# A two-layer hybrid decoder trunk: the attention layer's loop over heads cut at another place, and the delta-rule layer without its products with the zero state

## The chip, the core and the metric

The kernel runs on one core of one Trainium2 chip. The metric is the device time of one execution in microseconds; the median of three runs is compared. One further execution was profiled, and all rows shown come from it.

## The reference

The input is 1024 tokens of width 1024, all float32. Two layers are computed, each of the form x = x + mixer(rms_norm(x)). Layer 0 is a gated delta rule with 8 heads (key width 128, value width 256): per head a state S of 128 x 256 runs over the sequence, and the first chunk starts from a state of zeros.

```python
def step(state, inp):
    q_c, k_c, u_c, w_c, g_c, qk_c = inp
    v_new = u_c - jnp.einsum("bhck,bhkv->bhcv", w_c, state)
    o = (jnp.einsum("bhck,bhkv->bhcv", q_c * jnp.exp(g_c)[..., None], state)
         + jnp.einsum("bhij,bhjv->bhiv", qk_c, v_new))
    state = (state * jnp.exp(g_last)[..., None]
             + jnp.einsum("bhck,bhcv->bhkv", k_c * ..., v_new))
    return state, o
state0 = jnp.zeros((Bn, H, DK, DV), f32)
```

Layer 1 is attention with 8 heads in three groups each (dilations 1, 4, 16; a window of 128 earlier keys in the dilated stream). Queries and keys are normalised and rotated, and the three groups of a position are merged by their softmax denominators, multiplied by silu(z), and projected out.

## The kernel before

The program runs in stages, one after the other: constants; the norm of layer 0; `delta_heads`; `out_projection` (p0); the norm of layer 1; `attention_heads`; `out_projection` (p1). Names in the trace carry the stage's letter: a_ for the delta-rule heads, b_ for the attention heads, p_ for the output projections. Float32 products of the projections are made of three products of rounded halves (`three_passes`, L336): high weight by high and by low activation, low weight by high activation.

In both head stages each engine has its own instruction list, written by a function `body(m, n)` that is called once for every head: in one body the projections of head n are made, and beside them the mixing of head m = n - 1, whose projections the body before made. The body is cut into slots (`for s in range(...)`). A slot holds a third of a half: 8 of the 24 matmuls that project 512 tokens for one unit of 128 columns. What else an engine does in a slot is fixed by tests on s. The first body has no head m, the last has no head n; those between are a hardware loop.

**Delta-rule heads.** A head has 8 tiles of 128 tokens, T = 8. Tile t takes slots 7 + 3t to 9 + 3t (`CHAIN0` = 7). In the first slot TensorE makes two products with the state (L754, into `step`), VectorE makes the residual `r` (L920) and ScalarE keeps the product with the query (`o1`, L622). In the second TensorE makes `new` (L763), and ScalarE makes `vn` (L627). In the third TensorE makes the state's update (L767, `kd` by `vn`) and the output within the tile (L768), and VectorE makes the next state (L929) and the output (L934). After the last tile VectorE clears the state (L927). Between them stand the steps of a block inverse (`first`, L850; `lev`, L857), for which GpSimd makes `um` (L537).

**Attention heads.** A head has 10 units (B_UNITS): a query and a key unit for each of three groups (units 0 to 5, 12 halves), three value units (6 to 8) and the gate z (unit 9). A body has 60 slots of projection. A query/key half q is projected in slots 3q to 3q + 2 and then goes through ScalarE and VectorE: ScalarE copies and squares it (L1483, L1485, L1488) in slot 3q + 3, VectorE splits the squares (`sq_lo`, L1706) and rotates in slot 3q + 4, TensorE sums the squares (L1609) at the end of slot 3q + 5, ScalarE makes the root in slot 3q + 6, and VectorE scales the half (`qk`, L1742) in slot 3q + 7. TensorE's list waits in its place: its sum of half q waits for `sq_lo` of that half.

For head m the same body has:

- slots 0 to 11: 12 pairs of score tiles on TensorE (L1568, into three buffers `ring`), and on VectorE for each tile the mask and the row maximum (L1659);
- slot 12: SyncE sends the maxima of two groups through device memory (`maxima`, L1388 to L1394) to bring them into token order; slot 17: VectorE joins them (L1665), SyncE sends them back (L1398 to L1402);
- slots 22 to 33: 24 exponentials on ScalarE (L1457), two in a slot;
- from slot 25 (`BATCH0`), every second slot: one of nine batches of transposes of the exponentials (L1588), a slot later the copy out of `ring` (`keep_batch`: ScalarE L1366 for even batches, VectorE L1368 for odd ones), and a slot later the product with the values (L1537, into `num`); at the end eight more products (L1547);
- slot 34: SyncE sends the denominators through device memory (L1413, L1415, wait, L1419); slot 37: VectorE joins them (L1677, waits for the transfer); slots 38 to 43: logarithm, a row broadcast back, the exponential of the gate;
- slots 37 and 47: numerator by z (L1688); slots 44 and 48: times the gate (L1694), and the store to `b_out`.

The lists are strict: whatever stands behind a waiting instruction on its engine waits too. The output projection p1 reads `b_out`, and its first product (L1149) comes after the whole attention stage is done and the first tiles have been loaded and split.

## Time and profile before

| | us |
|---|---|
| median of 3 runs (lowest, highest) | 2504.26 (2500.49, 2508.04) |
| the profiled execution, its time | 2505.46 |
| its span from first to last instruction | 2503.8 |
| TensorE matmuls busy in the span | 2369.3 (95%) |
| VectorE, ScalarE, GpSimd busy | 1431.0, 1262.5, 231.3 |
| mean granted TensorE clock | 0.977 |

The time of the profiled execution is 1.7 us more than its span, and 1.2 us above the median of the runs. Where the rows say "x24" or "x48" behind a TensorE instruction, it counts records: a product of full float32 operands leaves two records, a product of rounded ones one. A record's own length overlaps with the next one's, so what a matmul costs in a full queue is the distance between two starts. "[0.78 <-DVE b_kept L1368]" behind a row says how long its engine stood idle before it, and who ended that.

### The profile page before, as it was taken

How to read it: one execution, taken by the hardware profiler on the slowest of the kernel's cores; microseconds unless marked ns; L12 is line 12 of the kernel's file. 1: busy time of each engine (PE TensorE's matmuls, PEld its weight loads, DVE VectorE, ACT ScalarE, POOL GpSimd, SP SyncE). 2: the span in 40 equal slices, each digit the busy share in tenths (PEclk: the TensorE clock that was granted, in tenths of full speed). 3: DMA queues.
4: the chain of work that ended last, by engine and by line, in shares of the span. 5: the costliest groups of instructions: out<-in, count | busy, mean ns of one | idle time of the engine just before them, and what ended most of it. 6: DMA issues, size and time to landing. Idle time of an engine off the chain costs nothing. (4 is left out here: it accounts for less than half of the span.)

```text
span 2503.8 us, 35785 instructions
## 1 busy us (share of the span) xinstructions
PE 2369.3 (95%) x11662; PEld 1970.8 (79%) x11662; DVE 1431.0 (57%) x2632; ACT 1262.5 (50%) x2557; POOL 231.3 (9%) x387
## 2 busy tenths in 40 slices
PE   6999999999999997899699999999999999999679
PEld 5778788887878885688588888888888888888567
DVE  4756666575757563775573727364563727365145
ACT  4546565565555554444553636355463636355333
POOL 1021120202020220820000000000000000000000
PEclk9999999999999998899899999999999999999779
DMA  3121121303021211877311121111111121111067
GB/s 112 33 57 49 49 55 54 80 20 82 26 71 40 59 41 35 279 259 255 126 43 35 35 64 37 56 37 51 33 48 45 34 60 41 52 41 51 9 220 268
DMA packets 282432, 190.47 MB, mean 76 GB/s; under 512 B 72204, under 2 KB 260772, under 8 KB 282308
## 3 DMA queue, kind: packets, MB, share of 16 engines
q1 hardware_dynamic: 282308, 188.93, 25.5%
q8 instruction: 65, 1.06, 0.2%
q14 instruction: 59, 0.48, 0.1%
HBM read 161.43 MB, written 27.46 MB: 75 GB/s over the span
## 5 line engine op out<-in xcount | busy, mean ns | idle before, releaser
L336 PE MATMUL b_proj<-g_h_hi,wb_w_hi 128*128 128x512 f32 x1280 | 511.4, 400 | 5.0 <-PEq L234 5.0
L336 PE MATMUL b_proj<-g_h_lo,wb_w_hi 128*128 128x512 f32 x1280 | 508.9, 398 | 1.0
L336 PE MATMUL b_proj<-g_h_hi,wb_w_lo 128*128 128x512 f32 x1280 | 509.3, 398 | 0.0
L336 PE MATMUL a_proj<-g_h_hi,wa_w_hi 128*128 128x512 f32 x784 | 324.3, 414 | 7.4 <-PEq L234 6.1
L336 PE MATMUL a_proj<-g_h_lo,wa_w_hi 128*128 128x512 f32 x784 | 323.4, 413 | 0.0
L336 PE MATMUL a_proj<-g_h_hi,wa_w_lo 128*128 128x512 f32 x784 | 318.2, 406 | 0.0
L336 PEld LDWEIGHTS b_proj<-g_h_hi,wb_w_hi 128*128 128x128 f32 x1280 | 241.4, 189 | 54.0 <-issue 5.2
L336 PEld LDWEIGHTS b_proj<-g_h_lo,wb_w_hi 128*128 128x128 f32 x1280 | 241.2, 188 | 51.1 <-issue 1.8
L336 PEld LDWEIGHTS b_proj<-g_h_hi,wb_w_lo 128*128 128x128 f32 x1280 | 241.3, 188 | 49.4
L1642 DVE TENSOR_TENSOR wb_w_lo<-wb_raw,wb_w_hi 128x1024 fp32r<-128x1024 f32 x80 | 97.1, 1214 | 216.3 <-ACT wb_w_hi L1443 216.3
L1483 ACT ACTIVATE b_acc<-b_proj,g_gains 128x512 f32<-128x512 f32 x96 | 66.0, 688 | 272.8 <-PE b_proj L336 143.5
L336 PEld LDWEIGHTS a_proj<-g_h_hi,wa_w_hi 128*128 128x128 f32 x784 | 149.1, 190 | 38.6 <-issue 7.9
L1149 PE MATMUL p_y<-p_w_hi,p_a_hi 128*128 128x512 f32 x384 | 151.3, 394 | 23.5 <-DVE p_w_lo L1116 23.5
L336 PEld LDWEIGHTS a_proj<-g_h_lo,wa_w_hi 128*128 128x128 f32 x784 | 149.0, 190 | 30.5 <-issue 1.0
L336 PEld LDWEIGHTS a_proj<-g_h_hi,wa_w_lo 128*128 128x128 f32 x784 | 148.8, 190 | 28.9
L1149 PE MATMUL p_y<-p_w_lo,p_a_hi 128*128 128x512 f32 x384 | 150.6, 392 | 0.0
L1149 PE MATMUL p_y<-p_w_hi,p_a_lo 128*128 128x512 f32 x384 | 150.4, 392 | 0.0
L974 DVE SCALAR_TENSOR_TENSOR a_acc<-a_x_raw,a_hw,a_acc 128x512 f32<-128x512 f32 x192 | 144.3, 752 | 6.8
L1116 DVE TENSOR_TENSOR p_w_lo<-p_w_raw,p_w_hi 128x1024 fp32r<-128x1024 f32 x96 | 126.6, 1318 | 0.0
L1706 DVE TENSOR_TENSOR b_sq_lo<-b_sg,b_sq_hi 128x512 fp32r<-128x512 f32 x96 | 66.3, 691 | 92.2 <-ACT b_sq_hi L1488 92.2
L1104 ACT ACTIVATE p_a_hi<-p_a_raw 128x256 fp32r<-128x256 f32 x96 | 40.2, 418 | 141.1 <-PE p_y L1149 96.9
L1149 PEld LDWEIGHTS p_y<-p_w_hi,p_a_hi 128*128 128x128 f32 x384 | 72.9, 190 | 39.9 <-DVE p_w_lo L1116 24.7
(227 smaller groups left out, 4279.0 us busy)
## 6 DMA issues: line engine op xcount, KB each, us to landing
wb_raw<-in_b_w_in_dram SPq DMA_DIRECT2D x82, 512.0 KB, 3.8
p_w_raw<-in_a_w_out_dram SPq DMA_DIRECT2D x64, 512.0 KB, 3.8
wa_raw<-in_a_w_in_dram SPq DMA_DIRECT2D x48, 512.0 KB, 4.4
p_w_raw<-in_b_w_out_dram SPq DMA_DIRECT2D x32, 512.0 KB, 4.3
a_out<-a_og SPq DMA_DIRECT2D x64, 128.0 KB, 1.8
p_a_raw<-a_out SPq DMA_DIRECT2D x64, 128.0 KB, 4.6
a_zx<-inverse_tiles SPq DMA_DIRECT2D x16, 384.0 KB, 4.3
u_tiles<-a_u SPq DMA_DIRECT2D x8, 512.0 KB, 3.2
```

What stands on the lines that cost most here:

```text
L336: last = pe.matmul(out, w[:, k, :], a[:, k, ks], start=(n == 0), stop=(n == 23))
L974: ins = dve.scalar_tensor_tensor(acc[:, half], src, w, acc[:, half], ALU.mult, ALU.add)
L1104: act.activation(a_hi[c][:, :], a_raw[:, c, :], ACT.Copy).then_inc(high, 1)
L1116: dve.tensor_tensor(w_lo[c][:, :], w_raw[:, c, :], w_hi[c][:, :].bitcast(F32), ALU.subtract).then_inc(low, 1)
L1149: mm = pe.matmul(y[part % 2][b][:, :], a_[c][:, ts], w_[c][:, ns], start=(first and c == 0 and n == 0), stop=(last and c == RING - 1 and n ...
L1483: act.activation(acc[:, half], proj[half][:, :], ACT.Copy, scale=r.gains[:, gain:gain + 1]).then_inc(rope, 1)
L1642: dve.tensor_tensor(w_lo[slot_of(j)][:, :, :], raw[:, slot_of(j)], w_hi[slot_of(j)][:, :, :].bitcast(F32), ALU.subtract).then_inc(w_low, 1)
L1706: dve.tensor_tensor(sq_lo[:, :], sg[:, q % 2], sq_hi[:, :].bitcast(F32), ALU.subtract).then_inc(sq_low, 1)
```

## The change

There are two edits; `out_projection` is the same in both kernels.

1. Delta-rule heads: for tile 0 of a head the state is zero. Its two products with the state, VectorE's `r` and ScalarE's `o1` are gone; `new` is made from v itself, the next state is a copy of the update, and the output is a copy of the product within the tile. After tile 7, whose state nobody reads, the state's update (`kd` by `vn`) and the clearing of the state are gone too.

2. Attention heads: the body is cut elsewhere. Of its 60 slots the first 24 now project the value and gate units of head m (`LATE` = 4 units), and the last 36 the query and key units of head n. The first body projects only in its last 36 slots, the last body only in its first 24. The other work moves with it: score pairs 0 to 7 of head n stand in slots 52 to 59, pairs 8 to 11 of the same head in slots 5 to 8 of the next body; the maxima leave in slot 0, are joined in slot 9; exponentials in slots 13 to 24; batches from slot 16; denominators leave in slot 25, are joined in slot 28; the numerators are taken in slots 28 and 38, the gate in 35 and 39. The steps of a query/key half that fall behind slot 59 stand in the first slots of the next body. Bodies of 66 slots (`B_DELAYED`) become bodies of 60.

```diff
@@ -746,9 +746,9 @@
                     if m is not None:
                         t, k = divmod(s - CHAIN0, 3)
                         if 0 <= t < T:
-                            if k == 0:
-
-                                pe.wait_ge(st_s, m * T + (t + 1))
+                            if k == 0 and t:
+
+                                pe.wait_ge(st_s, m * (T - 1) + t)
                                 pe.wait_ge(o_s, m * T + (t + 2))
                                 for c in range(2):
                                     last = pe.matmul(step[:, c], kq[:, pm, t, c], state[:, t % 2, :],
@@ -756,15 +756,23 @@
                                 last.then_inc(ks_mm, 1)
                             if k == 1:
 
-                                pe.wait_ge(r_s, m * T + (t + 1))
+                                if t:
+                                    pe.wait_ge(r_s, m * (T - 1) + t)
+                                else:
+                                    pe.wait_ge(v_kept, m * 4 + 4)
                                 if t % 2 == 0:
                                     pe.wait_ge(lv_s, m * (LEVELS * T // 2) + (LEVELS * (t // 2 + 1) + 1))
                                 pe.wait_ge(vn_s, m * T + (t + 1))
-                                pe.matmul(new[:, :], zf[:, t], r[:, :], start=True, stop=True).then_inc(xr_mm, 1)
+                                pe.matmul(new[:, :], zf[:, t], r[:, :] if t else v[:, pm, 0, :], start=True, stop=True
+                                          ).then_inc(xr_mm, 1)
                             if k == 2:
                                 pe.wait_ge(vn_s, m * T + (t + 1 + 1))
-                                pe.wait_ge(o1_s, m * T + (t + 1 + 1))
-                                pe.matmul(step[:, 1], kd[:, t], vn[:, :], start=True, stop=True)
+                                if t:
+                                    pe.wait_ge(o1_s, m * (T - 1) + (t + 1))
+                                else:
+                                    pe.wait_ge(o_s, m * T + 2)
+                                if t < T - 1:
+                                    pe.matmul(step[:, 1], kd[:, t], vn[:, :], start=True, stop=True)
                                 pe.matmul(step[:, 0], attn[:, pm, t], vn[:, :], start=True, stop=True
                                           ).then_inc(osu_mm, 1)
                         t, k = divmod(s - CHAIN0 - 6, 3)
                         t, k = divmod(s - CHAIN0, 3)
-                        if 0 <= t < T and k == 0:
-                            dve.wait_ge(ks_mm, m * T + (t + 1))
+                        if 1 <= t < T and k == 0:
+                            dve.wait_ge(ks_mm, m * (T - 1) + t)
                             dve.scalar_tensor_tensor(r[:, :], step[:, 0], hc[:, pm, C_NEXP, t:t + 1], v[:, pm, t, :],
                                                      ALU.mult, ALU.add).then_inc(r_s, 1)
                         if 0 <= t < T and k == 2:
                             dve.wait_ge(osu_mm, m * T + (t + 1 + 1))
-                            dve.wait_ge(st_s, m * T + (t + 1))
-                            if t == T - 1:
-
-                                dve.memset(state[:, 0, :], 0.0).then_inc(st_s, 1)
-                            else:
+                            if t == 0:
+                                dve.tensor_copy(state[:, 1, :], step[:, 1]).then_inc(st_s, 1)
+                            elif t < T - 1:
+                                dve.wait_ge(st_s, m * (T - 1) + t)
                                 dve.scalar_tensor_tensor(state[:, (t + 1) % 2, :], state[:, t % 2, :],
                                                          hc[:, pm, C_LAST, t:t + 1], step[:, 1],
                                                          ALU.mult, ALU.add).then_inc(st_s, 1)
-                            dve.wait_ge(o1_s, m * T + (t + 2))
                             dve.wait_ge(o_mm, m * T + (t - 1 + 2))
-                            dve.tensor_tensor(o[:, t % 2, :], step[:, 0], o1[:, t % 2, :], ALU.add).then_inc(o_s, 1)
+                            if t:
+                                dve.wait_ge(o1_s, m * (T - 1) + (t + 1))
+                                dve.tensor_tensor(o[:, t % 2, :], step[:, 0], o1[:, t % 2, :], ALU.add).then_inc(o_s, 1)
+                            else:
+                                dve.tensor_copy(o[:, 0, :], step[:, 0]).then_inc(o_s, 1)
...
@@ -1156,13 +1165,26 @@
 B_UNITS = 3 * NG + 1
 B_HALVES = 2 * B_UNITS
 B_SLOTS = 3 * B_HALVES
-B_DELAYED = B_SLOTS + 6
+LATE = B_UNITS - 2 * NG
+SPLIT = 6 * LATE
+QK_WRAP = B_SLOTS - SPLIT
 SCORE = DK ** -0.5
 PAIRS = 12
 BATCHES = 9
-BATCH0 = 25
+EARLY_PAIRS = 8
+PAIRS_EARLY0 = B_SLOTS - EARLY_PAIRS
+PAIRS_LATE0 = 5
+MAX_OUT = 0
+MAX_JOIN = 9
+EXP0 = 13
+BATCH0 = 16
+DEN_OUT = 25
+DEN_JOIN = 28
+LN_OUT = 29
+GATE_ADD = 33
+GATE_EXP = 34
 NUMERATED = (BATCH0 + 12, BATCH0 + 22)
-FINISH = (44, 48)
+FINISH = (35, 39)
...
-        V_TURNS = tuple(3 * (13 + 2 * g) + 4 + c for g in range(NG) for c in range(2))
+        V_TURNS = tuple(3 * (2 * g + 1) + 4 + c for g in range(NG) for c in range(2))
+
+
+        def unit_of(m, n, u):
+
+            if u < LATE:
+                return m, 2 * NG + u
+            if u < B_UNITS:
+                return n, u - LATE
+            return n, 2 * NG + u - B_UNITS
+
+        def half_of(m, n, q):
+
+            if 0 <= q < 2 * LATE:
+                return m, 4 * NG + q
+            if 2 * LATE <= q < B_HALVES:
+                return n, q - 2 * LATE
+            return None, 0
+
+        def qk_at(m, n, s, delay):
+
+            for head, at in ((m, s + QK_WRAP), (n, s - SPLIT)):
+                q, k = divmod(at - delay, 3)
+                if head is not None and k == 0 and 0 <= q < 4 * NG and at >= 0:
+                    yield head, q
+
+        def pair_at(m, n, s):
+
+            if n is not None and 0 <= s - PAIRS_EARLY0 < EARLY_PAIRS:
+                return n, s - PAIRS_EARLY0
+            if m is not None and EARLY_PAIRS <= s - PAIRS_LATE0 + EARLY_PAIRS < PAIRS:
+                return m, s - PAIRS_LATE0 + EARLY_PAIRS
+            return None, 0
 
         def keep_batch(eng, m, i):
...
-                    if n is not None and s < B_SLOTS and s % 6 == 3:
-                        j = s // 6 + 2
-                        if j < B_UNITS:
-                            load(n, j)
-                        elif not last:
-                            load(n + 1, j - B_UNITS)
-                    if m is not None and s == 34:
+                    if s % 6 == 3:
+                        head, j = unit_of(m, n, s // 6 + 2)
+                        if head is not None and unit_of(m, n, s // 6)[0] is not None:
+                            load(head, j)
...
-                        if 22 <= s < 34:
-                            if s == 22:
+                        if EXP0 <= s < EXP0 + PAIRS:
+                            if s == EXP0:
                                 act.wait_ge(nb_in, m * 32 + 32)
                                 act.wait_ge(den_sum, m * 2 + 1)
-                            for g, tile in order[2 * (s - 22):2 * (s - 22) + 2]:
+                            for g, tile in order[2 * (s - EXP0):2 * (s - EXP0) + 2]:
...
+                    if s % 6 == 2:
+                        head, j = unit_of(m, n, s // 6 + 1)
+                        if head is not None and unit_of(m, n, s // 6)[0] is not None:
+                            split_high(head, j, not some(head) and j == 1)
...
+                    head, i = pair_at(m, n, s)
+                    if head is not None:
+                        if i % 4 == 0:
+                            pe.wait_ge(qkn, head * 12 + (4 * (i // 4) + 4 + 2))
+                        if i < 3:
+
+                            pe.wait_ge(p_kept[0], head * 5 + 1)
+                            pe.wait_ge(p_kept[1], head * 4 + 1)
+                        else:
+                            pe.wait_ge(mxs, head * (NG * T) + 2 * (i - 2))
+                        for c in range(2):
+                            g, tile, at, first, width, before = score_tiles[2 * i + c]
+                            begin = first - P if before else first
+                            mm = pe.matmul(ring[i % 3][:, c * 2 * P:c * 2 * P + width],
+                                           qk[:, 2 * g, first:first + P],
+                                           qk[:, 2 * g + 1, begin:begin + width], start=True, stop=True)
+                        mm.then_inc(score_mm, 1)
...
+                    q, third = divmod(s, 3)
+                    head, q = half_of(m, n, q)
+                    if head is not None:
                         j, half = divmod(q, 2)
                         if third == 0:
-                            pe.wait_ge(w_low, n * B_UNITS + (j + 1))
-                            if q > 1 or some(n):
...
-                        if s == 37:
+                        if s == DEN_JOIN:
...
                             dve.wait_ge(half_mm, m * 2 + (half + 1))
                             dve.wait_ge(o_stored, m * 32 + 16)
+                            dve.wait_ge(evac, m * B_HALVES + B_HALVES)
```

**The order on TensorE in the last attention head**, where projections end. b_proj is the projection, b_ring<-b_qk a score tile, b_ring<-g_ident,b_sc a batch of transposes, b_num a product with the values. Before:

```order
L1568 MATMUL b_ring<-b_qk 128x128
L1568 MATMUL b_ring<-b_qk 128x256 x7
L1568 MATMUL b_ring<-b_qk 128x128 x4
L1568 MATMUL b_ring<-b_qk 128x256 x4
L1568 MATMUL b_ring<-b_qk 128x128 x8
L1588 MATMUL b_ring<-g_ident,b_sc 128x128 x4
L1537 MATMUL b_num<-b_kept,b_v 128x128 x4
L1588 MATMUL b_ring<-g_ident,b_sc 128x128 x3
L1537 MATMUL b_num<-b_kept,b_v 128x128 x3
L1588 MATMUL b_ring<-g_ident,b_sc 128x128 x4
```

And in the changed kernel:

```order
L336 MATMUL b_proj<-g_h_hi,wb_w_hi 128x512
L336 MATMUL b_proj<-g_h_lo,wb_w_hi 128x512
L336 MATMUL b_proj<-g_h_hi,wb_w_lo 128x512
L1584 MATMUL b_num<-b_pairs_kept,b_v 128x64 x4
L1636 MATMUL b_ring<-g_ident,b_sc 128x128 x4
L1584 MATMUL b_num<-b_pairs_kept,b_v 128x64 x4
L1636 MATMUL b_ring<-g_ident,b_sc 128x128 x4
L1584 MATMUL b_num<-b_kept,b_v 128x128 x4
L1636 MATMUL b_ring<-g_ident,b_sc 128x128 x4
```

Before, all scores and all nine batches come behind the last projection; now the last projection has the scores and the batches 0 to 3 ahead of it, and batches 4 to 8 behind it.

**The order on VectorE in the last attention head**, from the joining of the maxima (b_mo) to the first numerator (b_fin). b_kept is the copy of an odd batch, b_den_by the joining of the denominators. Before:

```order
L1665 TENSOR_TENSOR b_mo<-b_mo 128x8
L1667 TENSOR_TENSOR b_mo<-b_mo,b_mx 128x8
L1671 TENSOR_SCALAR b_nb<-b_mo 128x8
L1368 COPY b_kept<-b_ring 128x384
L1368 COPY b_pairs_kept<-b_ring 128x512
L1368 COPY b_kept<-b_ring 128x512
L1677 TENSOR_TENSOR b_den_by<-b_den_by 128x8
L1679 TENSOR_TENSOR b_den_by<-b_den_by,b_den 128x8
L1688 TENSOR_TENSOR b_fin<-b_num,b_z 128x512
L1368 COPY b_kept<-b_ring 128x512
```

And in the changed kernel:

```order
L1712 TENSOR_TENSOR b_mo<-b_mo 128x8
L1714 TENSOR_TENSOR b_mo<-b_mo,b_mx 128x8
L1718 TENSOR_SCALAR b_nb<-b_mo 128x8
L1690 TENSOR_TENSOR wb_w_lo<-wb_raw,wb_w_hi 128x1024 x2
L1422 COPY b_kept<-b_ring 128x384
L1792 TENSOR_SCALAR b_zl<-b_z 128x512
L1422 COPY b_pairs_kept<-b_ring 128x512
L1792 TENSOR_SCALAR b_zl<-b_z 128x512
L1422 COPY b_kept<-b_ring 128x512
L1724 TENSOR_TENSOR b_den_by<-b_den_by 128x8
L1726 TENSOR_TENSOR b_den_by<-b_den_by,b_den 128x8
L1736 TENSOR_TENSOR b_fin<-b_num,b_z 128x512
```

The copy of batch 5 stands ahead of the joining of the denominators, and the copy of batch 7 behind it, as before; splits of weights (wb_w_lo) and the gate's argument (b_zl) have come between.

**The order on VectorE in the attention loop**, where score tiles are masked (ISA b_sc,b_mx, and b_mx its maximum). Before, the first pairs of a body:

```order
L1654 ISA
L1659 ISA b_sc,b_mx<-b_ring,g_band_mask 128x128
L1659 ISA b_mx 128x1
L1659 ISA b_sc,b_mx<-b_ring,g_band_mask 128x256
L1659 ISA b_mx 128x1
L1654 REGISTER_ALU
L1659 ISA b_sc,b_mx<-b_ring,g_band_mask 128x256
L1659 ISA b_mx 128x1
```

In the changed kernel, a piece from the last slots of the loop's body:

```order
L1705 ISA b_sc,b_mx<-b_ring,g_band_mask 128x256
L1705 ISA b_mx 128x1
L1705 ISA b_sc,b_mx<-b_ring,g_band_mask 128x256
L1705 ISA b_mx 128x1
L1749 REGISTER_ALU
L1750 TENSOR_TENSOR b_sq_lo<-b_sg,b_sq_hi 128x512
L1757 REGISTER_ALU
L1762 STREAM_SHUFFLE b_swap<-b_acc 32x512
L1763 REGISTER_ALU
L1764 TENSOR_TENSOR b_swap<-b_swap,t_sin 32x512
L1765 TENSOR_TENSOR b_acc<-b_acc,t_cos 32x512
L1766 REGISTER_ALU
```

Before, pairs 0 to 3 follow each other with nothing of the query/key work between them; now all eight early pairs lie among the splits, rotations and scalings of the query/key halves.

## Rows read from the trace of the kernel before

**Rows 1.** The page, busy tenths in 40 slices of the span: TensorE and its granted clock

```profile
PE   6999999999999997899699999999999999999679
...
PEclk9999999999999998899899999999999999999779
```

**Rows 2.** Waits, TensorE alone, 160 to 925 us: total us, times, longest

```profile
PE a_first L850 <- DVE a_zx L913: 7.6, 6, 1.3
```

**Rows 3.** Waits, all engines, 1225 to 2335 us

```profile
DVE b_den_by L1677 <- DMA b_den_by<-denominators: 23.6, 7, 4.1
```

**Rows 4.** Timeline, TensorE, delta-rule heads in the loop: start us, recorded us

```profile
350.76 0.60 PE L767 MATMUL a_step<-a_vn,a_kd 128*128 128x256 f32 x2
351.19 0.59 PE L768 MATMUL a_step<-a_vn,a_attn 128*128 128x256 f32 x2
```

**Rows 5.** Timeline, last delta-rule head, around its first tile

```profile
954.19 1.81 POOL L537 TENSOR_TENSOR a_um<-a_u,g_level_mask 128x768 f32<-128x768 f32 x1 [15.19 <-PE a_first L850]
...
955.59 1.91 PE L754 MATMUL a_step<-a_state,a_kq 128*128 128x256 f32 x4
...
957.30 1.06 PE L850 MATMUL a_first<-a_zx,a_um 128*128 128x128 f32 x4
...
958.15 0.69 PE L763 MATMUL a_new<-a_r,a_zf 128*128 128x256 f32 x2
```

**Rows 6.** Timeline, last attention head, all engines

```profile
2334.61 0.39 PE L336 MATMUL b_proj<-g_h_hi,wb_w_lo 128*128 128x512 f32 x1
2334.84 8.60 PE L1568 MATMUL b_ring<-b_qk 128*128 128x128 f32 x48
...
2361.32 0.40 ACT L1457 ACTIVATE b_sc<-b_sc,b_nb 128x128 f32<-128x128 f32 x1 [23.90 <-DMA b_nb<-maxima]
...
2375.66 0.36 SPq L1413 DMA_DIRECT2D denominators<-b_den  x1
...
2384.26 0.81 SPq L1419 DMA_DIRECT2D b_den_by<-denominators  x2
...
2387.28 0.17 DVE L1677 TENSOR_TENSOR b_den_by<-b_den_by 128x8 f32<-128x8 f32 x1 [3.04 <-DMA b_den_by<-denominators]
...
2390.93 0.69 DVE L1368 COPY b_kept<-b_ring 128x512 f32<-128x512 f32 x1 [2.68 <-PE b_ring L1588]
...
2391.68 2.08 PE L1537 MATMUL b_num<-b_kept,b_v 128*128 128x128 f32 x8 [0.78 <-DVE b_kept L1368]
...
2393.55 1.06 PE L1588 MATMUL b_ring<-g_ident,b_sc 128*128 128x128 f32 x4
...
2396.29 1.90 PE L1547 MATMUL b_num<-b_pairs_kept,b_v 128*128 128x64 f32 x16
...
2398.32 0.69 DVE L1688 TENSOR_TENSOR b_fin<-b_num,b_z 128x512 f32<-128x512 f32 x1 [1.40 <-PEq L1551]
...
2409.34 0.80 PE L1149 MATMUL p_y<-p_w_hi,p_a_hi 128*128 128x512 f32 x1 [11.15 <-DVE p_w_lo L1116]
```

**Rows 7.** Windows: span, PE, PEld, DVE, ACT, POOL busy, granted clock, DMA share, GB/s

```profile
2385.00:2390.00 5.00, 4.31 (x20) 3.91 (x20) 0.94 (x3) 0.69 (x2) 0.00 (x0) 0.50 0.05 2
```

**Rows 8.** Timeline, TensorE, attention heads in the loop

```profile
2196.32 1.02 PE L1568 MATMUL b_ring<-b_qk 128*128 128x256 f32 x4
...
2196.99 0.58 PE L336 MATMUL b_proj<-g_h_hi,wb_w_lo 128*128 128x512 f32 x1
...
2255.38 1.06 PE L1537 MATMUL b_num<-b_kept,b_v 128*128 128x128 f32 x8
...
2256.27 0.49 PE L1588 MATMUL b_ring<-g_ident,b_sc 128*128 128x128 f32 x3
```

**Rows 9.** Timeline, first attention body, its last query/key half

```profile
1304.29 0.69 DVE L1706 TENSOR_TENSOR b_sq_lo<-b_sg,b_sq_hi 128x512 fp32r<-128x512 f32 x1 [1.97 <-ACT b_sq_hi L1488]
...
1305.95 0.39 PE L1609 MATMUL b_side<-b_sq_hi,g_ones_r 128*128 128x512 f32 x1
...
1309.65 1.06 DVE L1742 TENSOR_TENSOR b_qk<-b_acc,b_sg 128x512 f32<-128x512 f32 x1
```

320 lines of the change are left out of this document (144 added, 176 removed).

## The prediction

> **What bounds the kernel now.** I read the page's busy tenths first. TensorE stands at 9 in nearly every slice and its granted clock with it; the exceptions are the first slice, the places where one stage ends and the next begins, and above all slices 38 and 39 (from 2316 to 2441 us), with 6 and 7 for the busy share and 7 and 7 for the clock [rows 1]. So there are two kinds of time. Inside the two loops over heads TensorE's own list is the bound, and only instructions taken off that list shorten them. At the end of the attention stage it is a chain through all engines.
>
> The waits confirm the first kind. In 765 us of delta-rule heads TensorE's largest wait is 7.6 us, in six pieces [rows 2]. In the attention heads the wait worth knowing is one of VectorE: before the joining of the denominators it stands still for 23.6 us in seven bodies, at most 4.1 [rows 3]. Nobody pays for it now.
>
> The timeline of the last attention head shows the second kind. The last projection matmul starts at 2334.61, the scores follow 0.23 us later at 2334.84, the first exponential comes at 2361.32, and the output projection starts at 2409.34: 74.5 us from 2334.84, in which TensorE has little to do and runs at the lower level of its clock, 0.50 or 1.2 GHz [rows 6, 7].
>
> **The delta-rule edit.** Each head loses three products of TensorE: two with the state at tile 0, one update at tile 7. From the start of one such product to the start of the next is 351.19 - 350.76 = 0.43 us [rows 4]; the products with the state have the same shape. That is 1.29 us a head. Seven of the eight heads are mixed beside another head's projections, where TensorE is the bound: 7 x 1.29 = 9.0 us. What goes from VectorE and ScalarE there (a residual, a scaled copy, a clearing) lies beside work of TensorE and counts nothing; the copies that take the place of two operations count nothing either. The added wait for v comes behind slots of projection that end long after v is there.
>
> The last head is a chain. GpSimd's masks for the next pair of tiles are ready at 954.19 + 1.81 = 956.00, but the product with them starts at 957.30, behind the two products with the state, and `new` at 958.15, 0.85 after it [rows 5]. Without the two, the first can start at 956.0 and `new` at 956.85: 1.3 us. The dropped update of tile 7 stands ahead of the last output and gives 0.43 more. Together 1.7 us (bounds: 0.4 if another chain holds, 2.2).
>
> **The attention edit, in the loop.** Every body has the same work as before in 60 slots, so TensorE's list is as long, and I put the steady part at nothing. Its cover is thinner in two places, which I price as a rival below.
>
> **The attention edit, in the last head.** Let E be the time at which the last projection is done (2334.84 before). Two things change.
>
> First, work moves ahead of E, where TensorE is busy, so E comes later. The scores: two wide tiles take 2196.99 - 2196.32 = 0.67 us, so 0.335 each [rows 8]; 11 of the 24 are wide, 13 have half the columns, for which I take 0.22 (between 0.17, half, and 0.335, no less at all): 3.7 + 2.9 = 6.6 us, and the last head's own row bounds it from above with 8.6 [rows 6]. The products of batches 0 to 2: four tiles take 2256.27 - 2255.38 = 0.89 [rows 8], so 11 tiles 2.4. The transposes of batches 0 to 3: a batch is recorded with 0.49 for three [rows 8], which is an upper bound since records overlap; I take 0.35 each, 1.4. Sum 10.4 us (9.5 to 13).
>
> Second, what is left behind E is shorter. The exponentials took 2375.66 - 2361.32 = 14.3 us [rows 6]. They now stand in slots 13 to 24, where TensorE needs at least 12 slots of 8 x 0.23 = 1.84 us, 22 us, and ScalarE has few other things: they end at about E. What follows is a chain that the order of VectorE's list makes. The copy of batch 7 stands behind the joining of the denominators. Before, the denominators were there (2387.28) before batch 7 was due (2390.93), so this cost nothing [rows 6]. Now the batches have a lead of some four, and the denominators have not. From E: 0.2 to the store, 2384.26 - 2375.66 = 8.6 for its writes of single elements, 2387.28 - 2384.26 = 3.0 to bring them back, 0.35 for the two sums, 0.7 for the first numerator: the copy of batch 7 starts at E + 12.9. TensorE stands still for some microseconds ahead of it, so I leave the clock at 1.2 GHz for the rest. From that copy on everything is as before: 2409.34 - 2390.93 = 18.4 us to the first product of the output projection, with the products of batch 7, the transposes of batch 8, the last eight products and the last numerator at 2398.32 in between, and the stores and the first loads after it [rows 6]. The output projection starts at E + 31.3 instead of E + 74.5, and E is 10.4 later: 74.5 - 10.4 - 31.3 = **32.8 us** (27 to 37: exponentials later by 2 or scores at 8.6 on one side, the full clock for the last batches on the other).
>
> **The sum.** 9.0 + 1.7 + 32.8 = 43.5 us, against the profiled execution's own 2505.46: **2462.0 us**. That execution is 1.2 us above the median of the runs, which I leave inside the range. Of the quarter passes in the change's name nothing is in the diff: the output projection is the same, and costs the same.
>
> The 8.6 us are where the notes and the row part. The Trainium skill (DMA: Bandwidth & Descriptors, Anatomy of one DMA) gives a DMA a fixed cost of about 2.0 us plus its bytes at 436 GB/s, fitted on GpSimd's path. By that the 4 KB of one store would be back in about 2 us, and the sum would be that of the third rival, 2458; the row has 8.6, and the row is used.
>
> **Rivals.**
>
> *TensorE waits a little in every body.* Two places. (a) Pair 8 in slot 5 needs query/key half 11, whose sum TensorE makes at the end of slot 2. In the first body of the kernel before, VectorE split the last half by 1304.98, the sum started at 1305.95, and half 11 was finished at 1310.71 [rows 9]. Pair 8 would be reached after the sum (0.46) and two slots (3.67), at 1310.08: a wait of 0.6 us, or 5 us over eight heads. Against it: in the new order score pairs lie over the last halves, each lengthens TensorE's slot by up to 0.67, and on VectorE they fill the time in which it waits for ScalarE (1.97 in front of this split [rows 9]), so VectorE should catch up, not fall back. (b) In slot 28 VectorE waits for the denominators, 11.8 us after the exponentials, and behind that stands the split of the next head's first half, for which TensorE waits at the end of slot 29. From slot 24 to there TensorE has 6 x 1.84 + 3 x 0.89 + 3 x 0.35 = 14.8 us; the chain needs 0.2 + 11.6 + 0.35 + 0.7 = 12.9. The room is 2 us, and each microsecond beyond it costs 7. With 1 to 3 us a body, 7 to 21 us go back: 2469 to 2483, at 2 us 2476.
>
> *The loop loses more than the end gains.* The same place (b) at its worst: the joining comes so late that TensorE waits in each of seven bodies. From 43.5 / 7 = 6.2 us a body on, the kernel is slower than before. The transfer would have to take 6.2 + 1.9 = 8.1 us more than the 11.6 of the rows, for instance because SyncE, which now also waits in slot 0 for the maxima, comes late to the store. At 9 us a body the time is 2462 + 63 = 2525. Against it: VectorE's waits for it never exceeded 4.1 us [rows 3], and SyncE has no other blocking transfer within ten slots.
>
> *The denominators come early.* If their store took 2 us and not 8.6, the joining would stand in nobody's way, and the end would hang on the batches alone: TensorE and the copies would bring batch 7 some 4 us earlier. 2458 us. Against it: 8.6 in the last head [rows 6].
>
> *The delta-rule loop gives nothing*, because the products removed only uncover waits of the inverse's steps, of which six exist [rows 2]: 2462 + 10.7 = 2473. Against it: 7.6 us of waits in 765 us, and none is named for the state.
>
> **How the numbers follow.** Forecast as summed 0.75; small waits in every body 0.15; slower 0.03; early denominators 0.03; no gain in the delta-rule loop 0.04. A measurement of this kernel can tell about 0.3% (7.5 us) from no change. Range: down to 2456 for the forecast's best bounds (37 for the end, 2.2 for the last delta-rule head), up to 2474, which takes in its worst bounds (27, and the 5 us of place (a)) and half of the small-waits case; it leaves out the worse half of that case and the slower one, about 1 in 8 with some misjudged sizes. Faster 0.96, same 0.01, slower 0.03.
>
> **What would show it.** In the changed profile: in the delta-rule heads 24 products, 48 records, fewer with the state and for its update, and the stage's end 10 to 11 us earlier; the period of attention bodies unchanged; the last projection matmul 10 us behind where it would stand otherwise; TensorE idle in front of batch 7's product, ended by VectorE's copy; VectorE's wait for b_den_by in the last head some 5 us. It is wrong if TensorE's waits in the attention loop name b_sq_lo or b_qk with more than 5 us in total, or if the output projection starts later than E + 36.

## The result, and the profile after

The changed kernel takes 2480.46 us (median of 4 runs, 2474.93 to 2481.77), the kernel before 2504.95 beside it (2500.49 to 2508.04). The ratio is 0.9898, 95% interval 0.9884 to 0.9913: 25 us or 1.0% faster, 18 us short of the forecast 2462 and outside its range. Two later repeats of the changed kernel gave 2476.55 and 2478.62, with ratios of 0.9888 and 0.9891. The page of the changed kernel, busy tenths as in [rows 1]:

```profile
PE   6999999999999997799699999999999999999979
...
PEclk9999999999999998899899999999999999999979
```

Of the two low slices at the end of the attention stage, 38 and 39, one is left. The stages, from the timelines, in us ("E" is the start of what follows the last projection matmul, as in the prediction; the repeats are the runs e8 and e15 below):

| stretch | before | forecast | changed | its repeats |
|---|---|---|---|---|
| start to the first product of p0 | 1012.7 | 1002.0 | 1009.0 | 1009.0, 1007.8 |
| to the first projection of attention | 214.9 | 214.9 | 213.5 | 212.8, 213.0 |
| to E | 1107.3 | 1117.7 | 1126.0 | 1125.6, 1124.7 |
| E to the first product of p1 | 74.5 | 31.3 | 34.2 | 32.8, 33.9 |
| to the end of the span | 94.5 | 94.5 | 95.9 | 95.0, 95.2 |

So against the forecast 7.0 us are missing up to p0, 8.3 in the attention loop, 2.9 in its last head and 1.4 in p1, and the stretch between the two loops was 1.4 us shorter, which nobody had forecast. That is 18.2 us; the spans differ from the forecast by 18.4, the rest is rounding.

**The delta-rule loop.** ScalarE's first vn of head 0 and of head 6 in the changed kernel, some waits of its TensorE from 160 to 925 us (total us, times, longest), and the turn of head 0 that follows the dropped update:

```profile
166.60 0.48 ACT L627 ACTIVATE a_vn<-a_new,a_hc 128x256 f32<-128x256 f32 x1
...
844.39 0.48 ACT L627 ACTIVATE a_vn<-a_new,a_hc 128x256 f32<-128x256 f32 x1
```

```profile
PE a_turn L783 <- ACT a_v L691: 2.0, 6, 0.3
PE a_first L858 <- DMA a_zx<-inverse_tiles: 1.1, 4, 0.5
```

```profile
247.58 0.41 PE L783 MATMUL a_turn<-g_ident,a_o 128*128 128x128 f32 x2 [0.34 <-ACT a_v L691]
```

The same three rows of the kernel before:

```profile
166.68 0.48 ACT L627 ACTIVATE a_vn<-a_new,a_hc 128x256 f32<-128x256 f32 x1
...
247.65 0.41 PE L775 MATMUL a_turn<-g_ident,a_o 128*128 128x128 f32 x2
...
850.05 0.47 ACT L627 ACTIVATE a_vn<-a_new,a_hc 128x256 f32<-128x256 f32 x1
```

Six heads take 677.8 us instead of 683.4, 5.6 less where 6 x 1.29 = 7.7 were forecast. In the thirteen profiles with the whole edit and this order the six take 676.7 to 679.9, in two without it 683.4 and 681.0: 4.5 us between the means.

The turn, which follows the dropped update, starts where it did: ScalarE's copy into a_v is now its releaser, with 0.34 us in every head. This place can be read without the scatter of the whole loop. From ScalarE's vn of tile 7 (242.74 us in the changed kernel's head 0, 242.81 before) to that turn pass 4.83 to 4.85 us in each of six heads of all sixteen profiles with this order, with the update or without it. So the dropped update is worth nothing. The gain of a head lies from its last turn, which follows 5.8 us later in all of them, to the next head's first vn, where the two products with the state are gone: 157.3 us over six heads on average against 161.8, 4.5 less where 6 x 0.86 = 5.2 were forecast, and single profiles lie between 156.3 and 159.5.

**The last delta-rule head** waits for the inverse's way through DRAM (device memory). Changed, then before:

```profile
933.09 0.67 SPq L496 DMA_DIRECT2D inverse_tiles<-a_bx  x1
...
937.30 1.99 SPq L500 DMA_DIRECT2D a_zx<-inverse_tiles  x4
...
940.01 1.22 PE L858 MATMUL a_first<-a_zx,a_um 128*128 128x128 f32 x4 [4.38 <-DMA a_zx<-inverse_tiles]
...
953.35 1.06 PE L766 MATMUL a_new<-a_v,a_zf 128*128 128x256 f32 x2
```

```profile
938.74 0.67 SPq L496 DMA_DIRECT2D inverse_tiles<-a_bx  x1
...
941.39 1.99 SPq L500 DMA_DIRECT2D a_zx<-inverse_tiles  x4
...
944.15 0.86 PE L850 MATMUL a_first<-a_zx,a_um 128*128 128x128 f32 x4 [2.87 <-DMA a_zx<-inverse_tiles]
```

From the second store to the first load were 4.2 us instead of 2.65, so of the 5.7 us won by then 4.1 were left; new came 4.8 us earlier and p0 3.6. The long gap does not come with the edit: of the fifteen profiles that have the edit or most of it, six have exactly 2.65 (e4, e5, e9 to e12) and nine 3.8 to 4.5. What makes it long is not shown.

**The attention loop.** A body is longer. One transposing of a batch that stands once in each body, in two bodies in a row, in the changed kernel and in the one before:

```profile
1504.82 0.65 PE L1636 MATMUL b_ring<-g_ident,b_sc 128*128 128x128 f32 x4 [0.31 <-PE b_num L1584]
...
1646.57 0.65 PE L1636 MATMUL b_ring<-g_ident,b_sc 128*128 128x128 f32 x4 [0.28 <-PE b_num L1584]
```

```profile
1572.65 0.65 PE L1588 MATMUL b_ring<-g_ident,b_sc 128*128 128x128 f32 x4 [0.28 <-PE b_num L1537]
...
1713.67 0.65 PE L1588 MATMUL b_ring<-g_ident,b_sc 128*128 128x128 f32 x4 [0.28 <-PE b_num L1537]
```

141.74 us (141.74 to 141.77 in the six distances between bodies) against 141.02: 0.72 in each of eight heads is 5.8 us. The same attention code gave 141.68 in e8, 141.74 in e15 and 142.0 in e2, so 0.1 between two kernels means nothing here. The waits of the changed kernel from 1225 to 2335 us name 0.30 of the 0.72, that for b_kept (TensorE's other one, 2.0 in total, stood before too), and neither b_sq_lo nor b_qk for TensorE:

```profile
DVE b_den_by L1724 <- DMA b_den_by<-denominators: 18.8, 7, 3.6
...
PE b_num L1584 <- ACT b_kept L1420: 2.1, 7, 0.3
PE b_ring L1636 <- PE b_num L1584: 2.0, 7, 0.3
```

The loop also began with more time at the lower clock. Windows on TensorE (span, busy, granted clock, DMA share, GB/s), the changed kernel's from its first projection at 1222.6 and then the one before's from 1227.6:

```profile
1222.60:1225.00 2.40, 2.40 (x6) 0.50 0.53 156
...
1227.00:1229.00 2.00, 2.00 (x8) 0.69 0.81 239
```

```profile
1227.60:1230.00 2.40, 2.40 (x6) 0.56 0.50 147
1230.00:1232.00 2.00, 2.00 (x8) 0.68 0.29 85
```

The rows left out in the first pair (1225 to 1227 us) read 0.50 too. That is about 2 us longer at half speed, 1 us lost. Of the 18.7 us by which E moved, 11.9 remain for the work moved ahead of it (forecast 10.4); this is a remainder and was not measured by itself.

**The last head.** Timeline of the changed kernel from E to p1:

```profile
2347.98 0.36 SPq L1464 DMA_DIRECT2D denominators<-b_den  x1
...
2348.59 1.10 PE L1584 MATMUL b_num<-b_pairs_kept,b_v 64*128 64x64 f32 x8
...
2358.64 0.81 SPq L1470 DMA_DIRECT2D b_den_by<-denominators  x2
...
2360.67 0.17 DVE L1724 TENSOR_TENSOR b_den_by<-b_den_by 128x8 f32<-128x8 f32 x1 [6.92 <-DMA b_den_by<-denominators]
...
2361.59 0.68 DVE L1422 COPY b_kept<-b_ring 128x512 f32<-128x512 f32 x1
2362.32 2.07 PE L1584 MATMUL b_num<-b_kept,b_v 128*128 128x128 f32 x8 [2.56 <-DVE b_kept L1422]
...
2366.38 1.23 DVE L1730 TENSOR_TENSOR b_zl<-b_zl,b_ln_row 128x1024 f32<-128x1024 f32 x1 [4.11 <-DMA b_ln_row<-denominators]
...
2367.80 3.51 PE L1594 MATMUL b_num<-b_pairs_kept,b_v 128*128 128x64 f32 x16
2368.72 0.69 DVE L1742 TENSOR_TENSOR b_fin<-b_fin,b_zl 128x512 f32<-128x512 f32 x1 [1.12 <-ACT b_zl L1518]
...
2371.45 0.69 DVE L1736 TENSOR_TENSOR b_fin<-b_num,b_z 128x512 f32<-128x512 f32 x1 [2.03 <-DMA b_out<-b_fin]
...
2382.83 0.79 PE L1158 MATMUL p_y<-p_w_hi,p_a_hi 128*128 128x512 f32 x1 [11.51 <-DVE p_w_lo L1125]
```

The copy of batch 7 starts at E + 13.0 (forecast 12.9). What follows takes 21.2 us instead of the 18.4 of [rows 6]. The last products took 3.51 us at 1.2 GHz (granted clock 0.50 from 2356 us on), where before they took 1.90 [rows 6], at nearly the full clock. Window of the kernel before on TensorE, columns as above:

```profile
2395.00:2400.00 5.00, 2.89 (x24) 0.98 0.14 52
```

So the 18.4 us were measured with the fast clock at the end. The second numerator at 2371.45 really waited for them, though the row names a store: the only stores that its instruction waits for are those of earlier heads.

### The profile page after: what moved, and what is told of

Its sections match the earlier page's. It is cut to its first block and busy times, and to the rows that moved or that the text cites. A ratio compares the mean times of both kernels' runs of the same rounds, so it can differ in the third digit from the quotient of the medians.

```text
span 2478.7 us, 35640 instructions
## 1 busy us (share of the span) xinstructions
PE 2360.4 (95%) x11614; PEld 1961.2 (79%) x11614; DVE 1422.6 (57%) x2614; ACT 1255.3 (51%) x2548; POOL 232.2 (9%) x387
## 5 line engine op out<-in xcount | busy, mean ns | idle before, releaser
L1690 DVE TENSOR_TENSOR wb_w_lo<-wb_raw,wb_w_hi 128x1024 fp32r<-128x1024 f32 x79 | 95.9, 1215 | 139.8 <-ACT wb_w_hi L1494 139.8
```

What stands on the lines that cost most here:

```text
L1690: dve.tensor_tensor(w_lo[slot_of(j)][:, :, :], raw[:, slot_of(j)], w_hi[slot_of(j)][:, :, :].bitcast(F32), ALU.subtract).then_inc(w_low, 1)
```

## The experiments

The runs were made in four groups: e1 to e4, e5 to e8, e9 to e12, e13 to e15. Only the second and the fourth have a repeat of the changed kernel (e8: 2476.55, e15: 2478.62). In the other two only the ratio to the kernel before can be compared, and weakly: in the third group the kernel before took 2511.81 us, 5 to 7 more than in the others. Where whole times do not part two kernels, the profiles are read.

**One part at a time.** e1_delta_alone has the delta-rule edit and the attention layer of before, e2_rotation_alone the reverse.

> Only the delta-rule edit; the attention layer is that of the kernel before. By the prediction's step this is 10.7 us off the kernel before, 2494 us, with the first product of the output projection p0 10.7 us earlier. By the theory from the two traces it is 3 to 6 us off, 2499 to 2502: in the loop the dropped update of tile 7 gives nothing, since TensorE's last turn waits for ScalarE's copy into a_v in its place (0.33 to 0.34 us in each of seven heads), so 2 x 0.43 x 7 = 6.0 us are left; and what the last head gains in front of its chain goes partly to the wait for the inverse's DMA and to VectorE's wait for the store of a_og.

Measured: 2500.35 us against 2506.06, ratio 0.9984 (0.9972 to 0.9996), so 4.0 us (1 to 7; 5.7 between the medians) and not 10.7. Its first product of p0 is at 1009.05, 3.6 us earlier; its attention bodies have 141.02 to 141.06 us again.

> Only the rotated attention loop; the delta-rule layer is that of the kernel before. By the prediction's step this is 32.8 us off the kernel before, 2472 us. By the theory from the two traces it is about 21 us off, 2484: the period of an attention body is 141.74 us and not 141.02 (0.7 us in each of eight heads), and behind the last projection matmul stand 34 us instead of the 31.3 forecast, with the first product of p1 at 1.2 GHz for about 3 us longer.

Measured: 2483.73 us, ratio 0.9903 (0.9886 to 0.9921). In its profile the span is 20.3 us shorter than before; E to p1 takes 34.2 us, the bodies 141.9 to 142.2. By the runs it is 20 to 29 us off and not 32.8. The two parts add up to the whole within what the runs can tell.

**The update of tile 7, kept.**

```diff
-                                if t < T - 1:
-                                    pe.matmul(step[:, 1], kd[:, t], vn[:, :], start=True, stop=True)
+                                pe.matmul(step[:, 1], kd[:, t], vn[:, :], start=True, stop=True)
```

> The changed kernel, with the update of the state by tile 7 computed again (and read by nobody), so that only the two products with the zero state are gone. If each product taken off TensorE's list is worth its 0.43 us, the end of the delta-rule stage comes 7 x 0.43 = 3.0 us later than in the changed kernel, and 0.4 more for the last head. If the wait for a_v stands in its place, the delta-rule loop is as long as in the changed kernel within 0.7 us, TensorE's wait a_turn for ACT a_v (2.3 us in seven pieces) is gone from the waits, and the time is the changed kernel's, 2480.

Measured: 2479.09 us, ratio 0.9894 (0.9877 to 0.9911). Six heads take 678.9 us (165.34 to 844.25), inside the 676.7 to 679.9 with the update dropped, and p0 begins at 1006.9, earlier than in the changed kernel. The wait for a_v is gone, as expected; of the waits between 160 and 925 us the inverse's DMA has:

```profile
PE a_first L857 <- DMA a_zx<-inverse_tiles: 1.4, 3, 0.7
```

From the vn of tile 7 to the turn are 4.84 or 4.85 us in each of six heads, as without the update. So the update's whole price is given back to the wait.

**v first.** ScalarE's copy into a_v moved ahead of the copy of the projection's half.

```diff
+                        q, k = divmod(s - 9, 3)
+                        if 4 <= q < 8 and k == 0:
...
                         q, k = divmod(s - 3, 3)
                         if 0 <= q < HALVES and k == 0:
```

> The changed kernel with one order altered on ScalarE in the delta-rule heads: the copy of turned v into a_v stands ahead of the copy of the projection's half in its slot, not behind it, so it is 0.6 us earlier. Theory: that copy is what TensorE waits for (0.33 us in seven heads) where the dropped update of tile 7 should have gained; with the copy early, the wait is gone from the list and the delta-rule loop ends 2.3 to 3.0 us earlier than in the changed kernel (last projection of the stage at about 932.5 instead of 935.2). Rival: the later copies of the projections' halves hold TensorE instead, then nothing or a loss.

Measured: 2476.48 us, with the changed kernel at 2476.55 in the same group. The wait for a_v is gone, and the turn comes 4.36 us behind the vn of tile 7 and not 4.84, so here the dropped update does pay. But the loop is no shorter: six heads take 679.4 us, and the inverse's DMA holds TensorE instead.

```profile
PE a_first L859 <- DMA a_zx<-inverse_tiles: 6.7, 6, 2.9
```

That was 1.1 us in the changed kernel (0.5 and 1.9 in its repeats). The theory named the right wait and not the one behind it: in these heads TensorE's list is only just the longest chain. Whether the copy's new place or chance made the DMA late here, one profile cannot tell.

**What lengthens an attention body.**

```diff
-BATCH0 = 16
+BATCH0 = 17
```

> The changed kernel with transposes, copies and products of every score batch one slot later (BATCH0 from 16 to 17), the exponentials where they are. Theory: the 0.7 us that a body of the attention loop grew by are mostly TensorE waiting in front of batch 2's product (0.69 us between two starts instead of 0.24) for ScalarE's copy, which stands behind the exponentials of slot 21; a slot later the copy is out of the wait and the period of a body falls from 141.74 to about 141.3, 3 to 4 us in all, 2477. Rival: the growth is the list's own (other neighbours of the transposes, more switches), then the period stays 141.7 and the time 2480.

Measured: 2477.08 us, ratio 0.9884 (0.9867 to 0.99). The period fell to 141.28 us, as the theory said, and E stands 1121.1 us behind the first projection, 4.9 less. But E to p1 takes 38.2 us, 4.0 more: ScalarE's copy of batch 6, a slot later, now stands behind the logarithm, which waits for the join, and TensorE for the copy.

```profile
2355.45 0.21 ACT L1514 ACTIVATE b_ln_den<-b_den_by 128x8 f32<-128x8 f32 x1 [8.74 <-DVE b_den_by L1726]
2355.56 0.58 ACT L1420 ACTIVATE b_kept<-b_ring 128x512 f32<-128x512 f32 x1
...
2356.19 2.08 PE L1584 MATMUL b_num<-b_kept,b_v 128*128 128x128 f32 x8 [4.80 <-ACT b_kept L1420]
```

```diff
-MAX_JOIN = 9
-EXP0 = 13
-DEN_OUT = 25
+MAX_JOIN = 8
+EXP0 = 12
+DEN_OUT = 24
```

> The changed kernel with the exponentials, the maxima's join and the store of the denominators one slot earlier (EXP0 12, MAX_JOIN 8, DEN_OUT 24), the batches where they are. Theory: ScalarE then comes to its copy of batch 2 before TensorE needs it, as in the run with later batches, so the period falls from 141.7 to about 141.3 us (3 to 4 us in all); and in the last head the denominators' store starts a slot, about 2 us, earlier against the last projection, so the 33 to 34.6 us behind it become 31 to 33. Together 4 to 6 us below the changed kernel: 2472 to 2475. Rival: the exponentials now wait for the maxima's round trip through DRAM, and nothing is gained.

Measured: 2477.63 us, ratio 0.9859 (0.9838 to 0.9881). In the profile nothing of it came: the period is 141.74 and E to p1 34.6 us. (The joining of the denominators did begin 2.1 us earlier behind E than in e10 and e12 of its group, but the last products ran at 1.2 GHz, ended at E + 22.5 and held up the second output.) The timeline of the changed kernel, TensorE's and ScalarE's rows without the projections, shows why the exponentials' place did not matter:

```profile
1348.42 0.61 PE L1676 MATMUL b_side<-g_ident,b_v_raw 128*128 128x128 f32 x4
1349.06 0.60 ACT L1561 ACTIVATE b_v<-b_side 128x512 f32<-128x512 f32 x1 [1.08 <-PE b_side L1676]
1349.56 0.50 ACT L1507 ACTIVATE b_sc<-b_sc,b_nb 128x256 f32<-128x256 f32 x1
...
1350.05 0.50 ACT L1507 ACTIVATE b_sc<-b_sc,b_nb 128x256 f32<-128x256 f32 x1
...
1350.54 0.58 ACT L1420 ACTIVATE b_kept<-b_ring 128x512 f32<-128x512 f32 x1
...
1351.17 1.16 PE L1584 MATMUL b_num<-b_kept,b_v 128*128 128x128 f32 x8 [0.30 <-ACT b_kept L1420]
```

TensorE turns a piece of v at the end of slot 20. ScalarE waits for it, copies it, does the two exponentials of slot 21, whichever they are, and only then the copy of batch 2, which TensorE needs one slot after the turn.

```diff
+                        i, k = divmod(s - BATCH0 - 1, 2)
+                        if k == 0 and 0 <= i < BATCHES and i % 2 == 0:
+                            keep_batch(act, m, i)
                         if EXP0 <= s < EXP0 + PAIRS:
...
-                        i, k = divmod(s - BATCH0 - 1, 2)
-                        if k == 0 and 0 <= i < BATCHES and i % 2 == 0:
-                            keep_batch(act, m, i)
```

> The changed kernel with one order altered on ScalarE in the attention bodies: the copy of a score batch stands ahead of its slot's two exponentials, not behind them. Theory, after the run with earlier exponentials left the period at 141.74: TensorE waits for the copy of batch 2 in slot 22 because that copy stands behind ScalarE's copy of the last turned piece of v (which TensorE itself issues only at the end of slot 20) and then behind the two exponentials of slot 21, whichever they are. Ahead of them it starts 1.5 us earlier, TensorE's wait b_num for ACT b_kept (2.1 to 2.4 us) is gone, and the period is 141.3 us; nothing changes behind the last projection. 3 to 4 us below the changed kernel in the same group of runs. Rival: the period stays at 141.7, so that the growth of a body is the list's own.

> The changed kernel once more, as the measure for the two others: 2476 to 2481 by the two medians so far.

Measured: 2474.28 us, and 2478.62 for the changed kernel beside it; ratios to before 0.9873 (0.9856 to 0.9889) and 0.9891 (0.9875 to 0.9908). The whole times alone would not part them for certain. The period does: 141.10 us in the one, 141.74 in the other, and TensorE's wait for b_kept is gone. Of the copies that the edit moves, only those of batches 0 and 2 share a slot with exponentials. Timeline of e13:

```profile
1348.82 0.60 ACT L1561 ACTIVATE b_v<-b_side 128x512 f32<-128x512 f32 x1 [1.08 <-PE b_side L1676]
1349.32 0.59 ACT L1420 ACTIVATE b_kept<-b_ring 128x512 f32<-128x512 f32 x1
...
1350.47 1.05 PE L1584 MATMUL b_num<-b_kept,b_v 128*128 128x128 f32 x8
...
1503.36 0.65 PE L1636 MATMUL b_ring<-g_ident,b_sc 128*128 128x128 f32 x4 [0.31 <-PE b_num L1584]
...
1644.46 0.65 PE L1636 MATMUL b_ring<-g_ident,b_sc 128*128 128x128 f32 x4 [0.28 <-PE b_num L1584]
```

So 0.64 of the 0.72 us are the place of these copies, and the only wait that went is that for batch 2. The 0.08 left are within what equal attention code differs by. The waits showed 0.30 us a body; the distance between two bodies showed all.

**The end of the last head.** In e5_join_behind:

```diff
-DEN_JOIN = 28
-LN_OUT = 29
-GATE_ADD = 33
-GATE_EXP = 34
-FINISH = (35, 39)
+DEN_JOIN = 32
+LN_OUT = 33
+GATE_ADD = 37
+GATE_EXP = 38
+FINISH = (39, 43)
```

> The changed kernel with the joining of the denominators, and all that follows it, four slots later (join 32, logarithm 33, gate 37 and 38, outputs 39 and 43), so that VectorE's copy of batch 7 stands ahead of the join. By the prediction the copy waits only because it stands behind the join; it would start when its transposes are done, 1.7 us earlier in the last head, and the output projection about 2 us earlier: 2478 to 2479. If the denominators bound the end through another path (gate, exponential, first store), the copy is earlier and the output projection is not: 2480. The attention loop should keep its period of 141.74 us.

> The changed kernel itself once more, so that the others of this group are compared with it on the same chip: 2480 within 2 us. In its profile the attention bodies should again have a period of 141.7 us and the delta-rule stage should end near 935; what differs from the first profile (places at 1.2 GHz, the inverse's DMA) shows how much of a difference of 2 us between two profiles means nothing.

Measured: 2480.59 us against 2476.55 for the changed kernel. The copy of batch 7 is at E + 12.5, as soon as its transposes are done, so the prediction's reason for its wait was right; it is only 0.5 us earlier, and not 1.7, because TensorE ran at 1.2 GHz from 2352 us on here. But ScalarE's logarithm now stands behind the copy of batch 8, and the gate's sum comes at E + 21.8 instead of E + 17.8; p1 begins at E + 35.8. The denominators bound the end through the path of the gate, as the expectation's second case had it.

In e8, TensorE's clock stood at 1.00 from 2358 to 2370 us and the last products took 1.90 us. Still only 1.4 us of the last head went: the first output's multiplication at 2368.02 and the second at 2369.41 end the gate's path, and p1 begins 10.9 us behind.

The other profiles bear this out. In six of them (e3, e7, e8, e10, e12, e13) the last products took 1.90 us. There the joining of the denominators begins anywhere from E + 12.2 to E + 13.9, but p1 follows it by 19.8 to 20.6 us in all six. In the five with 3.5 us for the last products (the changed kernel, e2, e9, e11, e14) it follows by 21.8 to 22.8. So with the fast clock the gate's path alone sets the end, and with the slow one the batches end last and p1 comes 1 to 3 us later behind the join.

In e6 and e12 useless products keep TensorE busy (in e12 without the last entry):

```diff
+KEEP_BUSY = {24: 3, 26: 3, 28: 3, 30: 10, 32: 3, 35: 44}
+                            for _ in range(KEEP_BUSY.get(s, 0)):
+                                pe.matmul(side[:, :], r.ones_r[:, :], r.h_hi[:, 0, 0:HALF], start=True, stop=True)
```

> The changed kernel with useless products (a ones matrix with the input's high part, into a buffer that nobody reads afterwards) in TensorE's idle time behind the last projection of the last attention head: 3 in each of slots 24, 26, 28, 32, 10 in slot 30 and 44 behind the last real product. They stand where TensorE waits for a copy. Theory: the last head's end ran at 1.2 GHz because TensorE stood idle, which cost 1.6 us at its last sixteen products and about 1 us elsewhere in the chain, and the output projection then began 3 us at 1.2 GHz. Kept busy, it goes at 2.4 GHz: the granted clock reads 1.00 from 2356 on, and 3 to 5 us go, 2476. Rival: the clock does not follow these products, or they delay the chain by as much: 2480 or more.

> The changed kernel with useless products only in front of the last batches of the last head (3 in slots 24, 26, 28 and 32, 10 in slot 30), none behind the last real product. In the run that also had 44 behind it the batches were done 20.8 us behind the last projection, but the output projection began at 39.0. Theory: the 44 held up the stage's end; without them two chains end it, the batches at the full clock and the gate's chain (join, logarithm, its row through DRAM, sum, exponential, outputs) which is the longer one then, so the output projection begins 33 us behind the last projection, not 34.6 as in the changed kernel's first profile and not 31.3 as forecast. If only the batches' chain counted, it would be 31 or less.

Measured: 2481.10 us for e6 (changed kernel 2476.55) and 2477.52 for e12, with a ratio of 0.9864 (0.9847 to 0.9881) in its group. TensorE ran at 1.2 GHz for some 3 us only (behind its idle time in front of batch 7; in e8, without useless products, it was nearly 7), but p1 began at E + 38.7 and E + 34.0. In e6 the 44 useless products ended at 2376.5 and SyncE's first load of p1 followed at 2376.8: a stage ends only when every engine's list has. In e12 the denominators came back 1.8 us later than in the changed kernel (join at E + 13.9 instead of 12.1), and from there the gate's path to the second output took its 9.9 us; the last real products did not matter. The late denominators are not the useless products' doing: e10, in the same group and without them, has its join at E + 13.9 too.

**Output projections with a warm start.**

```diff
+            for _ in range(16):
+                pe.matmul(y[0][0][:, :], g.ones_r[:, :], g.h_hi[:, 0, 0:HALF], start=True, stop=True)
```

> The changed kernel with 16 useless products at the head of TensorE's list in both output projections, ahead of its wait for the first split weights. Theory: TensorE stands idle for 11 to 13 us there and starts the first real products at 1.2 GHz, for 3 to 5 us each; the useless products take that part. 2 to 5 us below the changed kernel, with the granted clock at 1.00 within 2 us of the first real product. Rival: the products end, the clock falls again before the weights are there, and nothing is gained; or the list is so late that the first real product waits for it.

> The two edits of the runs with earlier exponentials and with useless products ahead of the output projections together. They stand in different stages, so their gains should add: 6 to 10 us below the changed kernel, 2468 to 2472. If it is not below the better of the two by more than 2 us, one of them gives nothing.

> The last edit and the 16 useless products ahead of both output projections together, as a candidate that beats both kernels: from p0's and p1's first products to their ends 2 to 4 us less each, and the attention bodies at 141.3. 6 to 8 us below the changed kernel in the same group.

Measured: 2476.04 us for e10 (ratio 0.9860), 2474.98 for e11 (0.9855), 2474.08 for e14 (0.9870, beside 0.9873 for e13 and 0.9891 for the changed kernel). The clock did what the theory said. The useless products began at 1.2 GHz themselves, and in p0 of e10 they ended 2.65 us before the weights were there; but in all three runs and both projections the granted clock reads 1.00 at the first real product. Its rows in e10, with records of 0.50 us where the changed kernel has 0.79:

```profile
1008.60 0.50 PE L1161 MATMUL p_y<-p_w_hi,p_a_hi 128*128 128x512 f32 x1 [2.65 <-DVE p_w_lo L1125]
...
2381.60 0.50 PE L1161 MATMUL p_y<-p_w_hi,p_a_hi 128*128 128x512 f32 x1 [0.92 <-DVE p_w_lo L1125]
```

From the first real product of p1 to the end of the span these three take 93.1 to 93.3 us, all other profiles 94.4 to 95.9; from that of p0 to the attention stage 212.2 to 212.5, the others 212.8 to 216.3. So about 2 us go in p1 and perhaps as much in p0. Less of it reaches the whole. From E to the end of the span e10 takes 127.8 us, e11 126.7, e14 128.1, the changed kernel 130.1, 127.8 and 129.2; from the last delta-rule projection to the first one of attention e10 takes 283.6 us, e11 284.0, e14 286.4, the changed kernel 286.7 to 288.4. And the whole times of e13 and e14, 2474.28 and 2474.08, do not part. e11's forecast of 6 to 10 us below the changed kernel cannot be tested in its group; its half with the earlier exponentials gave nothing. As the gain of the useless products does not show for certain in a whole time, the version to keep is e13.

## Why the prediction was wrong

The sign and the large term were right: the exponentials and batches ahead of E, and a gain at the end of the stage alone. Four steps took too much. Neither of the two signs by which the prediction would have called itself wrong appeared (no wait for b_sq_lo or b_qk, and p1 at E + 34.2, not behind E + 36): they watched the places that it had thought of.

*"Each head loses three products of TensorE ... 7 x 1.29 = 9.0".* Two of the three products were worth about their price (4.5 us in six heads for 5.2), and the third was worth nothing. The update's 0.43 us, 3.0 in seven heads, went to the wait for a_v, which appears at 0.34 as soon as the product is gone; the turn behind it starts where it did to 0.02 us, and in e3, with the update kept, it is there too. In all, six heads gave 4.5 us on average and not 7.7; the page has the 48 records fewer (11614 matmuls and not 11662), as forecast. The prediction had asked which waits exist; the question was which releaser stands less than 0.43 us behind TensorE.

*"Together 1.7 us" for the last delta-rule head.* Its own chain became shorter, but by 0.7 us and not 1.3 (new is 4.8 us earlier and the start before it 4.1). In front of it TensorE waits for a DMA (2.9 and 3.5 us in the two profiles without the edit, 2.9 to 4.7 in those with it), which cost 1.5 us of the loop's gain in this profile and does not always do so. At the end the last turn is 5.0 us earlier and the last a_og only 4.0: it stands behind the store of the one before it (VectorE waits 2.29 us, before 1.94), 1.6 us behind its turn in all thirteen profiles with the whole edit, 0.6 and 0.7 in the two without. So here too a wait took the dropped update's place. Another 0.4 us went in the first loads of p0.

*"I put the steady part at nothing".* It cost 5.8 us. The rival of small waits in every body was right in kind, with neither of its places: place (a) and place (b) never show. The place is slot 22, where a turned piece of v, two exponentials and a copy stand in a row on ScalarE between two instructions of TensorE one slot apart; e13 and e4 take it away in two ways, and 0.64 and 0.46 us of the 0.72 go. Both the turn's new slot (20) and the batches' (from 16) are in the diff; the prediction looked at neither against the other. 1.0 us more of the loop's 8.3 is the slow clock at its start, 1.5 the moved work.

*"From that copy on everything is as before: 18.4".* It was 21.2, in e8 19.4. Two things are in it. First, the prediction leaves the clock at 1.2 GHz, but the 18.4 it takes over were measured with the last products at 0.98 of the full clock; at 1.2 GHz these alone take 1.6 us more. Nor is its remark right that TensorE runs at the lower level in all of the 74.5 us: windows of the kernel before read 1.00 from 2335 to 2345 us and 0.98 from 2395 to 2400. Second, before, the join had begun 3.65 us ahead of the copy [rows 6]; now it is what the copy waits for, and with it the path join, logarithm, row through DRAM, sum, exponential, outputs moved behind the copy. It needs 9.4 us from the join to the second output (e8) and 10.9 more to p1, so p1 began at E + 32.4 at the earliest in all runs with this order, whatever TensorE's clock did. At 1.2 GHz the batches end 1 to 2 us behind it. The copy itself was right to 0.1 us, by luck: the stores took 10.7 us (forecast 8.6), but they began 0.6 us before E and not 0.2 behind it, and the way back took 2.0 (forecast 3.0). The trace of before could have warned: there the last head's stores took 8.6, but those of the other seven heads 8.5 to 10.8.

The moved work was 11.9 us for 10.4, inside its bounds, if the remainder is all its own. The full clock for the last batches, which was to be worth the 37 of the range, happened in e8 and gave 1.4. VectorE's wait for b_den_by in the last head was 6.9 us and not 5.

The third rival, denominators that come early, is refuted by the 10.7 us. The Trainium skill (DMA: Bandwidth & Descriptors, Anatomy of one DMA) has a fit, made on GpSimd's path, from which an estimate for 4 KB is 2.0 us. The DMA view of the changed kernel (KB each, median us from issue to landing) is near it where runs of 32 bytes are read back, and not for the two stores, one in single elements and one in runs of four:

```profile
denominators<-b_den SPq DMA_DIRECT2D x16, 4.0 KB, 9.6
b_den_by<-denominators SPq DMA_DIRECT2D x16, 4.0 KB, 1.7
```

The same page (Rules for kernel authors) says that a strided last dimension becomes one descriptor per element; that fits the first of the two stores, and no run here stored these numbers in another order.

## What to carry to other kernels

When work comes off a list that is full, look on every other engine for the releaser that is next in time at that place, and take the smaller of the two: 0.43 us removed were worth nothing to the turn behind it, where the wait that appeared is 0.34 us long. When slots are renumbered, check each buffer's copy against what its engine must do between the two neighbours that it joins, and measure the period between two bodies, since the waits showed 0.30 of 0.72 us. A stretch taken over from another trace brings the clock of that trace with it. Where a chain loses one limb, write down the other limb's length before calling the rest unchanged.
